# Depthwise convolution of a decoder trunk: products and sums, or matmuls with diagonal tiles

## The reference, cut to what matters

```python
def conv_mixer(a, prev, dw, dw_bias, ln_g, ln_b, pw):
    g = a[..., :CONV_W] * jax.nn.sigmoid(a[..., CONV_W:])
    buf = jnp.concatenate([prev.astype(g.dtype), g], axis=1)
    y = lax.conv_general_dilated(buf, dw[:, None, :].astype(g.dtype), window_strides=(1,),
                                 padding='VALID', dimension_numbers=('NWC', 'WIO', 'NWC'),
                                 feature_group_count=CONV_W) + dw_bias
    y = jax.nn.silu(layernorm(y, ln_g, ln_b)) @ pw
    return y, buf[:, -(CONV_K - 1):]
```

## Time and profile before

| what | us |
|---|---|
| runs of the kernel before, median (lowest, highest) | 1281.38 (1280.11, 1283.01) |
| span of the profiled execution, first to last instruction | 1277.1 |
| TensorE matmuls busy in it | 1132.0 (89%) |
| VectorE busy | 823.4 (64%) |
| ScalarE busy | 588.0 (46%) |
| GpSimd busy | 285.3 (22%) |

### The profile page before, as it was taken

One profiled execution on the slowest core, in us unless ns is written; L12 is line 12 of the kernel. 1 busy time (PEld: TensorE's weight loads), 2 busy tenths in 40 slices (PEclk: granted clock), 3 DMA queues, 4 the chain that ended last, 5 costly groups with the idle time before them and its releaser, 6 DMA issues.

```text
span 1277.1 us, 27125 instructions
## 1 busy us (share of the span) xinstructions
PE 1132.0 (89%) x8432; PEld 1054.8 (83%) x8432; DVE 823.4 (64%) x1261; ACT 588.0 (46%) x972; POOL 285.3 (22%) x275
## 2 busy tenths in 40 slices
PE   4999998986589799999889999989756789999996
PEld 4999998865258799999889999977633678999994
DVE  4666645799943766664566665468997357666546
ACT  4444434555343544443454444353725345444435
POOL 0121100246351222110031211020835403211002
PEclk9999999898779899999989999989887899999998
DMA  6455565241282155555435555544206533555541
GB/s 236 163 212 202 178 212 201 97 113 50 79 185 84 66 198 181 181 181 181 149 86 209 186 178 200 210 148 141 83 20 122 140 132 111 178 188 173 190 164 36
DMA packets 91926, 192.88 MB, mean 151 GB/s; under 512 B 11986, under 2 KB 50066, under 8 KB 91730
## 3 DMA queue, kind: packets, MB, share of 16 engines
q1 hardware_dynamic: 89874, 187.58, 44.7%
q0 software_dynamic: 1984, 4.47, 1.7%
HBM read 189.42 MB, written 2.59 MB: 150 GB/s over the span
## 4 chain that ended last, share of the span: by engine, by line
PE 44%; issue 39%; POOL 10%; DVE 2%; POOLq 2%; ACT 2%; DMA 1%; DVEq 0%; SPq 0%; ACTq 0%
PE PS L974 14%; PE PS L975 14%; PE PS L976 14%; POOL cacc L1351 7%; PE PS L1000 2%; POOLq L1364 1%; POOL h L1328 1%; DMA raw<-in_wts 1%; ACT w_hi L334 1%; DVE w_lo L547 1%; DVE wk L669 1%; POOL vx L1365 1%; POOLq L1365 0%; POOL pa L1370 0%; DVE rstd L582 0%
## 5 line engine op out<-in xcount | busy, mean ns | idle before, releaser
L547 DVE TENSOR_TENSOR w_lo<-raw,w_hi 128x1024 fp32r<-128x1024 f32 x312 | 411.4, 1319 | 319.2 <-ACT w_hi L334 317.3
L974 PE MATMUL PS<-x_hi,w_hi 128*128 128x264 f32 x1648 | 492.6, 299 | 9.9 <-DVE w_lo L547 9.9
L975 PE MATMUL PS<-x_lo,w_hi 128*128 128x264 f32 x1648 | 476.4, 289 | 0.0
L976 PE MATMUL PS<-x_hi,w_lo 128*128 128x264 f32 x1648 | 476.0, 289 | 0.0
L334 ACT ACTIVATE w_hi<-raw 128x1024 fp32r<-128x1024 f32 x312 | 328.2, 1054 | 232.0 <-PE PS L976 229.5
L974 PEld LDWEIGHTS PS<-x_hi,w_hi 128*128 128x128 f32 x1648 | 321.0, 195 | 14.2 <-DVE w_lo L547 10.7
L975 PEld LDWEIGHTS PS<-x_lo,w_hi 128*128 128x128 f32 x1648 | 320.7, 195 | 2.6
L976 PEld LDWEIGHTS PS<-x_hi,w_lo 128*128 128x128 f32 x1648 | 318.6, 193 | 0.0
L974 PE MATMUL PS<-h_hi,w_hi 128*128 (+1 forms) x832 | 237.4, 285 | 3.1 <-issue 3.1
L976 PE MATMUL PS<-h_hi,w_lo 128*128 (+1 forms) x832 | 237.1, 285 | 0.0
L975 PE MATMUL PS<-h_lo,w_hi 128*128 (+1 forms) x832 | 236.4, 284 | 0.0
(11 more groups left out here) (245 smaller groups left out, 1030.8 us busy)
## 6 DMA issues: line engine op xcount, KB each, us to landing
raw<-in_wts SPq DMA_DIRECT2D x315, 512.0 KB, 3.7
kv<-in_kT SPq DMA_DIRECT2D x128, 64.0 KB, 1.9
kx<-in_kxT SPq DMA_DIRECT2D x128, 32.0 KB, 2.1
kv<-in_vC SPq DMA_DIRECT2D x64, 64.0 KB, 7.1
vx<-in_vC SPq DMA_DIRECT2D x32, 64.0 KB, 2.0
vx<-in_vC POOLq DMA_DIRECT2D x32, 64.0 KB
h<-in_xT SPq DMA_DIRECT2D x1, 1056.0 KB, 4.8
out_yT<-h SPq DMA_DIRECT2D x8, 132.0 KB, 1.7
```

The lines of the kernel that those rows point to most:

```text
L547: tt(w_lo[:, u % SPLIT, :], raw[:, u % RAW, :], w_hi[:, u % SPLIT, :].bitcast(F32), AL.subtract).then_inc(sem["w_lo"], 1)
L974: pe.matmul(out, w_hi[:, w, cols], hi, start=start, stop=False)
L975: pe.matmul(out, w_hi[:, w, cols], lo, start=False, stop=False)
L976: return pe.matmul(out, w_lo[:, w, cols], hi, start=False, stop=stop)
```

## The change

ScalarE no longer multiplies the input. For each tap and half it multiplies the identity matrix by the tap's weights, which gives a 128x128 tile with the weights on its diagonal, in a ring of four taps (`PAIRS`, `diag`). TensorE multiplies this tile with the shifted input as a float32 matmul of 256 columns, 62 of them in a layer, accumulated in bank 7 of PSUM. ScalarE then adds the bias while it copies the bank to `cacc` (signal `conv_p`). GpSimd's 31 additions are gone.

The taps are spread over TensorE's program: 3 before unit 9, 3 after the transposes behind it, 2 after each of four permutations, 3 after unit 14, 5 before digit 6, 5 before digit 7 and 4 before `scores(0)`. Since bank 7 is taken, two permutations move to bank 3 and the transposed values to bank 6; with that TensorE waits for `v_nat` before digit 0. `equal` shares its place with `diag`, so `equals` waits for the last tap. In GpSimd's program the store of the indexer keys and the 16 DMAs into `vx` now come directly behind the stores of keys and values and a wait for unit 14, and the pooling stores and window sums come after them.

```diff
@@ -76,7 +79,7 @@
     s_p=4, s_masked=4, p_exp=4, p_norm=4, p_t=8, p_tc=8, o_p=4, o_hi=4, o_lo=4,
     s_s=1, s_smax=1, p_sexp=1, p_snorm=1, p_st=1, p_stc=1, k_used=8, v_used=8, o_sc=1, o_st=1, o_ms=1,
     o_shi=1, o_slo=1, dg=1,
-    tanh=2, glu=2, tap=CK, conv=CK, c_sum=1, c_cent=1, c_sq=1, c_var=1, c_rms=1, c_norm=1, c_silu=1,
+    tanh=2, glu=2, tap=CK, conv=CK, conv_p=1, c_sum=1, c_cent=1, c_sq=1, c_var=1, c_rms=1, c_norm=1, c_silu=1,
     c_hi=1, c_lo=1, c_out=1, c_ohi=1, c_olo=1,
     pool_x=1, pool_y=1, pl_hi=1, pl_lo=1, pl_ohi=1, pl_olo=1,
     step=400, pstep=60, astep=40,
@@ -158,6 +161,7 @@
         vn = place("vn", [128, 2, 128], F32, s2)
         kiw = place("kiw", [128, NT], F32, s2)
         equal = place("equal", [128, NS], F32, [s2[0]])
+        diag = place("diag", [128, 2 * PAIRS, 128], F32, [s2[0]])
         rd = place("rd", [32, NS], F32, s2)
         assert s2[0] <= s2_end
         Z = place("Z", [128, NS], F32)
@@ -399,19 +403,17 @@
 
                 taken = [0]
 
-                def taps(n):
-
-                    for k in range(taken[0], taken[0] + n):
-                        if k == 0:
-                            act.wait_ge(sem["glu"], at_layer(L, "glu", 2))
-                        if k >= 2:
-                            act.wait_ge(sem["conv"], at_layer(L, "conv", k - 1))
+                def taps(upto):
+
+                    for k in range(taken[0], upto):
+                        if k >= PAIRS:
+                            act.wait_ge(sem["conv"], at_layer(L, "conv", k - PAIRS + 1))
                         for c in range(2):
                             w = DW + CK * c + k
-                            ins = act.activation((cv, cg)[k % 2][:, c, 0:NP], gp[:, c, k:k + NP], ACT.Copy,
+                            ins = act.activation(diag[:, 2 * (k % PAIRS) + c, :], ident, ACT.Copy,
                                                  scale=pars[:, w:w + 1])
                         ins.then_inc(sem["tap"], 1)
-                    taken[0] += n
+                    taken[0] = upto
 
                 def tanh(c):
                     act.wait_ge(sem["chunk"], at_layer(L, "chunk", 5 + 2 * c))
@@ -437,21 +439,29 @@
                 act.wait_ge(sem["idx_s"], at_layer(L, "idx_s", 1))
                 act.activation(X[:, 0:PAST], PS[:, 4:6, :].rearrange("p a b -> p (a b)"), ACT.Copy)
                 act.activation(X[:, PAST:], PS[:, 6, 0:1], ACT.Copy).then_inc(sem["idx_x"], 1)
-                for m in range(10, 12):
+                taps(4)
+                split(L, u0 + 10)
+                split(L, u0 + 11)
+                act.wait_ge(sem["v_t"], at_layer(L, "v_t", 1))
+                act.activation(vn[:, :, :], PS[:, 6, 128:384].rearrange(
+                    "p (a b) -> p a b", a=2), ACT.Copy).then_inc(sem["v_nat"], 1)
+                taps(8)
+                for m, upto in ((12, 10), (13, 12), (14, 14), (15, 17), (16, 17), (17, 19)):
                     split(L, u0 + m)
-                    taps(3)
-                act.wait_ge(sem["v_t"], at_layer(L, "v_t", 1))
-                act.activation(vn[:, :, :], PS[:, 3, 0:256].rearrange(
-                    "p (a b) -> p a b", a=2), ACT.Copy).then_inc(sem["v_nat"], 1)
-                for m in range(12, 18):
-                    taps(3)
-                    split(L, u0 + m)
+                    taps(upto)
 
                 act.wait_ge(sem["chunk"], at_layer(L, "chunk", 15))
                 for c in range(2):
                     act.activation(pp[:, c, PB:], xp[:, c, 0:NP], ACT.Copy)
                     ins = act.activation(stp[:, c, :, PB], xp[:, c, NP:], ACT.Copy)
                 ins.then_inc(sem["pool_c"], 1)
+                taps(CK)
+
+                act.wait_ge(sem["conv"], at_layer(L, "conv", CK))
+                for c in range(2):
+                    ins = act.activation(cacc[:, c, 0:NP], PS[:, 7, NP * c:NP * c + NP], ACT.Identity,
+                                         bias=pars[:, DWB + c:DWB + c + 1])
+                ins.then_inc(sem["conv_p"], 1)
 
                 def exps(j):
                     act.wait_ge(sem["s_masked"], at_layer(L, "s_masked", j + 1))
@@ -467,8 +477,6 @@
                 for j in range(4):
                     if j < 3:
                         exps(j + 1)
-                    if j == 0:
-                        taps(CK - taken[0])
                     for a in range(2):
                         act.wait_ge(sem["p_t"], at_layer(L, "p_t", 2 * j + a + 1))
                         if j:
@@ -862,6 +870,8 @@
                     ts(room, cnt, -1.0, float(TOPK_S), AL.mult, AL.add)
 
                 def equals():
+
+                    dve.wait_ge(sem["conv"], at_layer(L, "conv", CK))
                     linked(ts(equal[:, :], X[:, :], thr, None, AL.is_equal))
                     return step(L, dve.tensor_tensor_scan(ties[:, :], equal[:, :], equal[:, :], 0.0, AL.add, AL.bypass))
@@ -1068,6 +1078,22 @@
                     pe.matmul(PS[:, 6, 448 + i:449 + i], con[:, C_OWN:C_OWN + 128], rad[:, 1:2],
                               start=True, stop=True).then_inc(sem["digit"], 1)
 
+                drawn = [0]
+
+                def taps(upto):
+
+                    for k in range(drawn[0], upto):
+                        if k == 0:
+                            pe.wait_ge(sem["glu"], at_layer(L, "glu", 2))
+                            pe.wait_ge(sem["idx_relu"], at_layer(L, "idx_relu", 4))
+                        pe.wait_ge(sem["tap"], at_layer(L, "tap", k + 1))
+                        for c in range(2):
+                            ins = pe.matmul(PS[:, 7, NP * c:NP * c + NP], diag[:, 2 * (k % PAIRS) + c, :],
+                                            gp[:, c, k:k + NP], start=(k == 0 and c == 0), stop=(k == CK - 1),
+                                            skip_group_check=True)
+                        ins.then_inc(sem["conv"], 1)
+                    drawn[0] = upto
+
                 first_units(L, 0, u0)
                 pe.wait_ge(tables, 64)
                 unit(2)
@@ -1117,31 +1143,39 @@
                     pe.matmul(PS[:, 4 + c, :], wx[:, :], rd[:, 512 * c:512 * c + 512], start=True, stop=True)
                 pe.matmul(PS[:, 6, 0:1], wx[:, :], rd[:, PAST:], start=True, stop=True).then_inc(sem["idx_s"], 1)
                 unit(8)
-                pe.wait_ge(sem["idx_relu"], at_layer(L, "idx_relu", 4))
-                perm(7, ak[:, :], 7).then_inc(sem["perm"], 1)
+                perm(7, ak[:, :], 3).then_inc(sem["perm"], 1)
+                taps(3)
                 unit(9)
 
                 pe.wait_ge(sem["chunk"], at_layer(L, "chunk", 9))
+                pe.wait_ge(sem["idx_x"], at_layer(L, "idx_x", 1))
                 for b in range(2):
-                    ins = pe.transpose(PS[:, 3, 128 * b:128 * b + 128], av[:, 128 * b:128 * b + 128], ident)
+                    ins = pe.transpose(PS[:, 6, 128 + 128 * b:256 + 128 * b], av[:, 128 * b:128 * b + 128], ident)
                 ins.then_inc(sem["v_t"], 1)
+                taps(6)
+                pe.wait_ge(sem["v_nat"], at_layer(L, "v_nat", 1))
                 digit(0)
                 unit(10)
                 perm(9, aq[:, 0, :], 2).then_inc(sem["perm"], 1)
+                taps(8)
                 digit(1)
                 unit(11)
                 pe.wait_ge(sem["rope"], at_layer(L, "rope", 4))
-                perm(10, aq[:, 1, :], 7).then_inc(sem["perm"], 1)
+                perm(10, aq[:, 1, :], 3).then_inc(sem["perm"], 1)
+                taps(10)
                 digit(2)
                 unit(12)
                 pe.wait_ge(sem["rope"], at_layer(L, "rope", 5))
                 perm(11, aq[:, 2, :], 2).then_inc(sem["perm"], 1)
+                taps(12)
                 digit(3)
                 unit(13)
-                pe.wait_ge(sem["v_nat"], at_layer(L, "v_nat", 1))
+                pe.wait_ge(sem["rope"], at_layer(L, "rope", 6))
                 perm(12, aq[:, 3, :], 3).then_inc(sem["perm"], 1)
+                taps(14)
                 digit(4)
                 unit(14)
+                taps(17)
 
                 def keys(b):
@@ -1172,8 +1206,11 @@
                 for b in range(KV):
                     keys(b)
                     if b == 1:
+                        taps(22)
                         digit(6)
+                taps(27)
                 digit(7)
+                taps(CK)
                 scores(0)
                 scores(1)
@@ -1182,7 +1219,10 @@
                     for a in range(2):
                         if j:
                             pe.wait_ge(sem["p_tc"], at_layer(L, "p_tc", 2 * j - 1 + a))
-                        elif a:
+                        elif a == 0:
+
+                            pe.wait_ge(sem["conv_p"], at_layer(L, "conv_p", 1))
+                        else:
 
                             pe.wait_ge(sem["chunk"], at_layer(L, "chunk", 15))
                         p = sp_[:, j % 2, a, :]
@@ -1208,7 +1248,7 @@
                 ins.then_inc(sem["s_s"], 1)
 
 
```

(27 more changed lines are left out.)

## The result

The changed kernel takes 1260.63 us (median of 4 runs, 1260.21 to 1261.93); the kernel before, run with it, 1282.08 (1280.11 to 1283.01). The ratio is 0.9839, 95% interval 0.9825 to 0.9852: 21 us faster. The forecast was 1262.

The account below looks back on a forecast made before the run. VectorE, inflated by GpSimd's additions, bounds the search; TensorE also stalls at the attention's start and at unit 15. Gains of 7.5 + 2.0 = 9.5 a layer, 19 for two, give 1281.4 - 19 = 1262 us, range 1253 to 1276.

Parts of the forecast that it names:

- Price of a tap: On TensorE: 0.43 us a float32 matmul of 256 columns, 0.86 a tap, 26.7 for 31 taps a layer.
- C: Cheap taps on TensorE: a diagonal matmul costs 0.22, VectorE bounds again, `masked(0)` 10 earlier than forecast, 1242; chance 0.05.
- Place 1: The search, first permutation to `masked(0)`: bound moves from VectorE to TensorE, 57.4 plus 0.7 idle; `masked(0)` 0.8 earlier.
- Clock: TensorE in the search: taps fill its gaps, so full clock, near 1.0 instead of 0.84, then 0.81.
- A: Cold taps: search clock stays about 0.8, 57.4 become 72, `masked(0)` 13.6 later than summed, 1289; chance 0.09.
- Place 2: The attention's start: TensorE's 6.78 stall before the values product goes, 7.6 gained there; 7.5 together, search included.
- The two terms behind it: Behind the values product: 0.6 gained from warmer TensorE and uninflated `chosen`; 0.7 charged for window sums on `norm(0)`, `equals`.
- Rival B: Collision moved: window sums meet VectorE's `norm(0)`, `norm(1)` and `chosen`, four a layer instead of 0.7, 1269; chance 0.13.
- Place 3: The end, unit 15: its 18 matmuls take 2.2 instead of 4.24, 2.0 gained.
- Sum: Both mixer layers: 7.5 + 2.0 = 9.5 a layer, 19 for two, time 1281.4 - 19 = 1262.
- D: Half the gain: TensorE taps at 0.46 with idle times of 1 to 2.5 each group, 6 a layer, 1274; chance 0.13.
- The bounds named for the range: Fast end: 0.3 for `v_nat`, 1.3 for the attention's start, no collision, taps at 0.40; 12.5 a layer, 1256.

Follow-up runs that it names:

- a_sums_first: Kernel after, with GpSimd's pooling stores and window sums ahead of its 16 value DMAs instead of behind them: 1254.42 us, ratio 0.9794.
- b_best: Kernel before, with ScalarE's last seven taps ahead of the first exponentials and SyncE's page numbers read earlier: 1260.60 us, ratio 0.9844.
- a_best2: Kernel after, window sums first, page numbers early, TensorE's last taps behind pair 0's scores, diagonals before `exps(0)`, PSUM copy before `exps(1)`: 1247.96 us, ratio 0.9743.
- b_one_tap: Kernel before with last taps ahead of the exponentials and page numbers earlier, cut to 1 of 31 taps: 1233.44 us, ratio 0.9631.
- a_pool_load: Kernel after, plus 31 unused GpSimd additions of 128x512 a layer, one behind each tap: 1276.14 us, ratio 0.9958.
- b_taps_early: Kernel before, with ScalarE's last seven taps ahead of the first exponentials instead of between them and the copies `pT`: 1270.12 us, ratio 0.9927.
- experiment 6: Kernel before, with ScalarE's last seven taps ahead of the first exponentials and SyncE's page numbers read earlier (b_best): 1260.60 us, ratio 0.9844.

## Why the prediction was right, step by step

The intervals of the first layer, each the difference of two starts in TensorE's timelines (last column: unit 15):

```
                first permutation   to unit 15   unit 15's
                to the values                    18 matmuls
before               78.63            35.32        4.24
after                70.92            34.92        2.39
forecast             71.0             35.4         2.2
a_sums_first         70.61            32.30        2.39
b_best               73.80            32.37        2.39
a_best2              63.79            35.24        2.38
b_one_tap            57.54            34.55        2.39
```

- **Price of a tap.** Right, with a small offset: 0.443 a matmul where I had 0.43, so 27.5 for the taps instead of 26.7. TensorE's own work came to 57.1 (57.4 forecast), so the rest of it was about 1 cheaper than I summed. C, the cheap tap, is out.
- **Place 1.** The bound moved to TensorE, as said, and the relief of VectorE (56.63 to 43.69, 12.9 where I had 14) was paid to the taps. `masked(0)` came 1.6 sooner after the permutation where I had 0.8; the 0.7 of idle time at the first digit did not come.
- **Clock.** The 1.00 is right, so A is out, but my reason was not the only one that does it. I said that the taps fill TensorE's gaps. They can: a_pool_load, with taps on TensorE and GpSimd adding, has 0.97 up to `masked(0)`. They are not needed: b_one_tap has none, and its search runs at 0.97 too, since VectorE, not slowed by additions, keeps TensorE fed. Only with the additions and without the taps is the clock low (0.86 in the search before, 0.81 in b_best). The Trainium skill, TensorE: Matmul & The Clock Gate, section What's actually happening, has the throttled state as the default and activity as what releases it; the traces agree in direction (0.81 in b_best, where TensorE waits for a slowed VectorE, 0.97 in b_one_tap, 1.00 in the kernel after). What a low clock in the search costs by itself no run shows.
- **Place 2.** The stall of 6.78 went, 7.7 gained at the product with the values (7.6 forecast). b_best shows that the part behind `masked(0)` was never TensorE's: from there to the product it takes 13.5 (73.80 less 60.33), the kernel after 13.6, the kernel before 19.7. The order of ScalarE's queue gives half of those 6 us (b_taps_early takes 16.6), the earlier keys the rest. What TensorE gives here is the search, 57.34 against 60.33.
- **The two terms behind it** are where the forecast was off, and they cancelled. I gave 0.6 for a warmer TensorE and heads without inflation and charged 0.7 for the window sums. a_sums_first shows the charge at 2.62, and then the first term is 35.32 - 32.30 = 3.0. Rival B's mechanism was real, at two thirds of its price (4 a layer); what it left out is that the kernel before had as much of its own in the same interval. The rule cited in B, that VectorE with two SBUF inputs and GpSimd reading SBUF exclude each other (the Trainium skill, SBUF — State Buffer, Who interferes with whom), fits the product by `sps` (1.03 to 2.13), and `masked`, which reads PSUM, stayed at 0.96. It fits the scan as well (2.30 to 2.70), which reads `equal` as both of its inputs. The equality test has one input from SBUF and lengthened too (0.75 to 1.11). The prediction said that with one input they do not exclude each other; the section says this only outside the modes in which VectorE uses two ports for one tensor, and it counts `tensor_scalar`, which this test is, among the operations that can enter them. Whether the test did so, no row shows.
- **Place 3.** 1.85 for 2.0. Every kernel here whose sums end before they are asked for has it, b_best too, so it belongs to GpSimd's lateness and not to the change.
- **Sum.** From the permutation on 9.96 in the first layer and 8.9 in the second, for 9.5 each. Ahead of the permutation the layers add +0.5 and -0.7; no run explains these.
- **Slips in the rivals and the range.** 57.4 at a clock of 0.8 are 72, which is 14.6 more and not 13.6, so A's time would be some 2 more than 1289. D's own idle times, 1 to 2.5 in each of 10 groups, come to more than the 6 a layer that it charges. The bounds named for the range add up to 13.2 a layer, not 12.5. The 1.15 a tap in A comes from no row. The result hangs on none of these.

What was missed is not in the sum but in its meaning. The forecast said that the search gains next to nothing since the taps take what VectorE gives, and left it there. The consequence is experiment 6: if the search gains 1.6 and the rest comes from an order, then an order is enough. b_best has the same time within the intervals (ratio 0.9844 against 0.9839). The move to TensorE pays once the order around it is right as well: 6.2 below b_best with the window sums first (a_sums_first), 12.6 with the page numbers early and the last taps where TensorE waits anyway (a_best2). Whether a better order could take more off b_best as well, no run tried.

Two loose ends. a_pool_load also pushed GpSimd's transfers by over 30 us (its additions end at 338.3, the sums at about 376), so its 15.5 need not be collisions alone; but 7.5 of the 7.7 that its first mixer lost are there before the product with the values, ahead of those transfers' use. And in a_best2 the values to unit 15 take 35.24: the product comes 6.8 earlier than in a_sums_first, but VectorE, without idle time from `masked(0)` on, copies the first heads only 4.4 earlier, starts of the permutation corrected (340.56 against 345.02). So VectorE looks like the next bound there; this is argued, since no run took anything off it.

## What to carry to other kernels

When work is moved to another engine, split the gain into what the new place gives and what the order gives, and try the order alone: here seven taps moved ahead of the exponentials and 48 page numbers read earlier gave as much as the whole change, 21 us. An engine that seems to have idle time before a wait (6.6 us here) has less of it than the row shows if others wait for its results along the way. After each step look for what comes 2 to 10 us behind: keys by DMA, window sums, and shared bytes were each hidden until the step ahead of them went.

## What the hardware showed that I had not expected

- Collisions between VectorE and GpSimd stretch GpSimd too: beside the scan (337.65 to 340.35) a copy that takes 0.39 in a_sums_first takes 2.30, from 338.24 to 340.54. The scan itself grew by 0.40.
- Cutting float32 matmuls from 256 to 128 columns saves nearly half of their time (ten of them in 2.33 instead of 4.43): little fixed share is seen at these sizes.
- 48 reads of page numbers hold SyncE's queue in the kernel after from 295.0 to 322.0, 0.56 each; spread behind the raw units they cost nothing that these runs show (1262.51 against 1260.63, intervals overlapping).
